# State-space decay exponents: one minimum over four chunks, the column subtracted as the exponential's bias

## The reference, cut to what matters

```python
a_cs = jnp.cumsum((dt * a)...)                   # running sum of the log decay
seg = a_cs[..., :, None] - a_cs[..., None, :]
decay = jnp.exp(jnp.where(causal, seg, -jnp.inf))
cb = jnp.einsum('bclgn,bcsgn->bcgls', cm, bm)
y_diag = jnp.einsum('bcgls,bcgjls,bcsgjp->bclgjp', cb, decay, xdt)
```

## Time and profile before

| | |
|---|---|
| median of 3 runs | 1905.43 us (1902.82 to 1907.98) |
| profiled execution, its own time | 1910.72 us |
| its span, first to last instruction | 1909.1 us |
| PE busy | 1687.8 us, 88% of the span |
| DVE busy | 728.6 us, 38% |
| ACT busy | 374.4 us, 20% |
| POOL busy | 278.9 us, 15% |
| mean granted TensorE clock | 0.951 |

### The profile page before, as it was taken

How to read it: one execution, slowest core, us unless ns; L and a number is a source line. 1 busy time by engine, 2 the same in 40 slices (tenths; PEclk the granted TensorE clock), 3 DMA queues, 4 the chain that set the end, 5 groups by cost and what they waited for, 6 DMA issues and landing times.

```text
span 1909.1 us, 22819 instructions
## 1 busy us (share of the span) xinstructions
PE 1687.8 (88%) x8856; PEld 900.1 (47%) x8857; DVE 728.6 (38%) x1292; ACT 374.4 (20%) x722; POOL 278.9 (15%) x300
## 2 busy tenths in 40 slices
PE   3989799899889889999999999999999867999893
PEld 0554455355355344544454555444656343555441
DVE  1144743754564464620014776214015221222124
ACT  2321232132122122000012333410010121111112
POOL 0003411430530341000000000000000012222122
PEclk9999899999899989999999999999989878999997
DMA  9621101021011116622111001213331645997994
GB/s 314 247 76 44 45 22 45 1 67 44 1 45 45 44 45 220 220 88 89 45 44 44 30 14 45 89 44 104 143 122 45 263 177 205 394 347 291 394 378 152
DMA packets 109537, 242.00 MB, mean 127 GB/s; under 512 B 8505, under 2 KB 18238, under 8 KB 109474
## 3 DMA queue, kind: packets, MB, share of 16 engines
q1 hardware_dynamic: 86800, 180.60, 26.3%
q0 software_dynamic: 14128, 48.51, 7.0%
q10 hardware_dynamic: 8546, 12.03, 1.8%
HBM read 219.10 MB, written 22.02 MB: 126 GB/s over the span
## 4 chain that ended last, share of the span: by engine, by line
PE 75%; DVE 12%; ACT 3%; DMA 3%; issue 3%; POOL 2%; ACTq 2%; DVEq 0%; POOLq 0%; PEldq 0%
PE psum L432 15%; PE psum L1036 8%; PE psum L444 7%; PE psum L722 6%; PE psum L609 4%; PE psum L1058 4%; PE psum L436 4%; PE psum L837 3%; PE psum L667 2%; PE psum L635 2%; PE psum L506 2%; PE psum L454 2%; PE psum L871 1%; PE psum L769 1%; DVE arena L1726 1%
## 5 line engine op out<-in xcount | busy, mean ns | idle before, releaser
L432 PE MATMUL psum<-arena 128*128 128x512 f32 x688 | 312.9, 611 | 10.3 <-issue 4.6
L432 PEld LDWEIGHTS psum<-arena 128*128 128x128 f32 x688 | 132.3, 196 | 171.1 <-issue 163.3
L1036 PE MATMUL psum<-arena 128*32 128x256 f32 x2816 | 166.9, 389 | 1.5 <-DVE arena L2080 1.5
L444 PE MATMUL psum<-arena 128*128 128x512 f32 x352 | 155.2, 600 | 0.1
L609 PE MATMUL psum<-arena 128*128 128x512 f32 x256 | 131.7, 645 | 1.2 <-ACT arena L1230 1.2
L1036 PEld LDWEIGHTS psum<-arena 128*32 128x32 f32 x2816 | 92.2, 111 | 61.2 <-issue 8.5
L722 PE MATMUL psum<-arena 128*128 128x512 f32 x256 | 111.5, 593 | 0.0
L444 PEld LDWEIGHTS psum<-arena 128*128 128x128 f32 x352 | 67.3, 193 | 82.3 <-issue 82.2
L2156 POOL TENSOR_TENSOR arena<-arena 128x512 f32<-128x512 f32 x40 | 49.5, 1248 | 356.5 <-ACT arena L1285 305.6
L2192 POOL TENSOR_TENSOR arena<-arena 128x512 f32<-128x512 f32 x64 | 82.7, 1296 | 101.7 <-ACT arena L1325 101.7
L1682 DVE SCALAR_TENSOR_TENSOR arena<-arena 128x772 f32<-128x772 f32 (+1 forms) x96 | 93.9, 978 | 3.4
(11 more groups left out here) (350 smaller groups left out, 2124.7 us busy)
## 6 DMA issues: line engine op xcount, KB each, us to landing
arena<-exp_w_d SPq DMA_DIRECT2D x48, 2048.0 KB, 17.7
arena<-w_in_d SPq DMA_DIRECT2D x22, 2048.0 KB, 7.9
arena<-ada_w_d POOLq DMA_DIRECT2D x8, 2048.0 KB, 9.1
slots<-arena POOLq DMA_DIRECT2D x1, 9216.0 KB, 27.2
arena<-ada_w_d SPq DMA_DIRECT2D x4, 2048.0 KB, 23.2
arena<-ssd_proj_d SPq DMA_DIRECT2D x4, 2048.0 KB, 9.5
slots<-arena POOLq DMA_DIRECT2D x92, 64.0 KB, 5.0
arena<-slots POOLq DMA_DIRECT2D x22, 256.0 KB, 6.1
```

The costliest lines, as they stand in the source:

```text
L432: ins = mmul(ps[:, 0:T], slot[:, k, m * P:(m + 1) * P], src[:, k, C:NT], start=(k == 0), stop=(k == KD - 1))
L444: ins = mmul(ps[:, 0:n], src[:, k, t * P:(t + 1) * P], slot[:, k, 0:n], start=(k == 0), stop=(k == KD - 1))
L1036: ins = mmul(psU[q * R:(q + 1) * R, 0:2 * HF], XT[:, k % 2, k // 2, :], w13[p][:, :, k, q * HF:(q + 1) * HF], start=(k == 0), stop=(k == K ...
```

## The change

DVE makes a negated copy of `acs` once, in `tmpd[0]` (`nacs`). For each head, DVE's four instructions become one, which takes the minimum of the row and the column, with the column broadcast along each chunk. The exponential adds the negated column as its bias: min(r, a) - a is min(r - a, 0). A bias is one number for each partition, and the four chunks have different ones, so ACT's one exponential of 512 columns becomes four of 128.

```diff
--- before.py
+++ after.py
@@ -154,6 +154,7 @@
         tmpd = [alloc(TT, 2 * SH) for _ in range(2)]
+        nacs = tmpd[0]
@@ -1322,7 +1323,10 @@
                         act.wait_ge(*is_free(("R", g, d, h)))
-                        run(mm[n % NM], mm[n % NM], ACT.Exp).then_inc(S_("decay_ready"), 1)
+                        at = d * SH + g * HPG + h
+                        for c in range(TL):
+                            ins = run(mm[n % NM][:, c, :], mm[n % NM][:, c, :], ACT.Exp, bias=nacs[:, TC + c, at:at + 1])
+                        ins.then_inc(S_("decay_ready"), 1)
@@ -1641,6 +1645,7 @@
             dve.wait_ge(*is_free(("acs",)))
+            step(v.tensor_scalar(nacs, acs, -1.0, None, ALU.mult))
             v.tensor_tensor(wend, tmpd[1], acs, ALU.subtract).then_inc(S_("acs_out"), 1)
@@ -1740,10 +1745,8 @@
-                    for c in range(TL):
-                        ins = v.tensor_scalar(mm[n % NM][:, c, :], bank(key)[:, c * P:(c + 1) * P],
-                                              acs[:, TC + c, at:at + 1], 0.0, ALU.subtract, ALU.min)
-                    ins.then_inc(is_free(key)[0], 1)
+                    v.tensor_tensor(mm[n % NM], bank(key)[:, :].rearrange("p (c l) -> p c l", c=TL),
+                                    acs[:, TC:TT, at:at + 1].to_broadcast([P, TL, P]), ALU.min).then_inc(is_free(key)[0], 1)
```

## The result

| | before | after |
|---|---|---|
| median of 5 runs | 1906.97 us (1902.82 to 1911.38) | 1921.55 us (1918.13 to 1923.15) |
| profiled execution, its own time | 1910.72 us | 1918.13 us |
| its span | 1909.1 us | 1916.5 us |
| DVE busy | 728.6 us | 691.6 us |
| ACT busy | 374.4 us | 414.2 us |

The changed kernel is slower: ratio 1.0066, with a 95% interval from 1.0048 to 1.0084. Two later sets of runs of the same kernel gave 1.0053 [1.0041, 1.0066] and 1.0062 [1.0038, 1.0087]. The forecast was 1907.0, in a range up to 1913. With the 1.6 us that it gave the change, some 9 to 13 us of the 10.9 to 14.6 measured are left that it had not put there.

What follows compares the result with a forecast made beforehand. PE was taken to bound the kernel, feeling the change only at 16 places where it waits. Four groups at +0.30 give +1.2 us, the negated copy +0.4: +1.6 on 1905.43, so 1907.0, range 1901 to 1913.

Steps and rivals of the forecast that it cites:

- The exponentials: ACT, each head: four exponentials of 128 columns take x = 1.29 us against 0.63, 0.66 more.
- that rival: ACT: the four exponentials don't overlap, x = 1.64, sum +7.2 us, 1912.6; chance 0.07.
- Place 1: First head of direction 0: ACT's table load hides the faster minimum, so PE waits 0.66 us more.
- Place 2: Middle of direction 0: the order at the ports turns round, PE's own loop keeps a head at 5.17 us; 0.
- the rival of the relief in the loop: DVE gives 0.44 us back in five heads of each group, 8.8 in all: 1898; chance 0.04.
- Place 3: Last head of direction 0: L1719 no longer stalled, 1.02 us less, chain 0.22 more: -0.80.
- Places 4 and 5: First and last head of direction 1: the longer chain is in the open, +0.22 us each.
- The negated copy: DVE, once, ahead of the split whose end PE waits for: +0.4 us in the open.
- each head's 0.22 reaches PE: Direction 0's middle loops are not closed by PE, 64 x 0.22 = 14 us: 1919.5; chance 0.03.
- the clock goes slower: In two or three groups a 1.2 GHz stretch is added outside cover, 1.8 to 2.7 us each: 1913; chance 0.06.
- the prediction's last sign of being wrong: Profile after: the prediction is wrong if the clock's stretches move.
- The clock goes faster: Moved waits leave the clock high after direction 0's first product, 10.8 us come back: 1896; chance 0.07.

Runs made afterwards that it cites:

- min_alone: Kernel before with DVE's one minimum, but one exponential of 512 columns without bias, so the column is not subtracted: 1898.22 us, 0.9940.
- after_twice_d1: Changed kernel, PE doing the product of the last head but one in direction 1 twice: 1921.93 us, 1.0074 against the kernel before.
- after_pause: Changed kernel, one part of the z projection moved from behind M(6) to behind M(0) in direction 0: 1922.95 us, 1.0055 against the kernel before.
- before_twice_d0: Kernel before, PE doing the product of the last head but one in direction 0 twice: 1912.12 us, 1.0017.
- before_late_first: Kernel before, one unused exponential of 512 columns added on ACT ahead of the first head of direction 0: 1912.66 us, 1.0015.
- before_z_three: Kernel before, three z projection parts ahead of direction 0's first product, none between its last two: 1900.93 us, 0.9962.
- after_z_three: Changed kernel, three z projection parts ahead of direction 0's first product, none between its last two: 1899.76 us, 0.9963 against the kernel before.
- z_three: Order of PE's work with three z projection parts ahead of direction 0's first product, in either kernel: 1900.93 us before the change, 1899.76 after.

## Why the prediction was wrong

Taken by its own steps:

- **DVE's minimum**, 0.69: right (690 ns), and it is not stalled beside POOL.
- **The exponentials**, x = 1.29 from 390 ns and 0.30 apart: 390 ns and 1.28. The overlap between neighbours in place is there; that rival is out. The Trainium skill ("ScalarE: Activation LUTs", What ACT_TABLE_LOAD costs) would give 387 ns and 1.27, and the trace agrees.
- **Place 1**, first head of direction 0, +0.66: from the row to M(0) the four groups took 16.96 and take 19.49, +0.63 a group.
- **Place 2**, the middle, 0: the order of the ports turned as described. The step from one L636 to the next is 5.09 (219.07 to 224.16), not 5.17, so PE's own loop was not quite what closed it; a moved step was one of the prediction's signs of being wrong. `min_alone` shows more of that: M(1) to M(6) lost 1.1 us a group, half of the 2.2 that the rival of the relief in the loop, at 0.04, had given. With the longer exponentials on top, the changed kernel gives none of it back at the end: M(1) to M(6) is 0.51 longer, as the product of the head before the last comes later.
- **Place 3**, last head of direction 0, -0.80: M(6) to M(7) is 1.46 shorter and M(1) to M(6) 0.51 longer, -0.95 together.
- **Places 4 and 5**, +0.22 each: +0.21 for the first; for the last +0.14 in the chain ahead of M(6) and 0.05 in M(6) to M(7), 0.2 together.
- **The negated copy**, +0.4: PE's wait ahead of the scan stage went from 4.3 to 4.7. In the view of waits of the changed kernel (name, count, the longest):

```profile
PE psum L559 <- DVE arena L1660: 4.7, 1, 4.7
```

The sum of these was +1.6; they measured +0.8 to +0.9. Had the time been made of them alone, it would have come out at 1908. So the rival "each head's 0.22 reaches PE" is out as well, though its 1919.5 lies near what was measured: it wanted 3.5 us of waits a group, and there are 0.1.

**The step that failed** is the rival "the clock goes slower", at 0.06 and with 1913 as its time, and behind it the sum of the forecast, which has no term for the clock: it puts at nothing, without a reason, that the stretches at 1.2 GHz could move. They did, by about 10 us of the 11, and the prediction's last sign of being wrong was just that. The rival's mechanism was put right, "if in two or three groups such a stretch is added outside cover": that is what happened, in three groups at the end of direction 1, and in M(0) to M(1) as well. But it was counted at 1.8 to 2.7 for each of two or three, and the open terms came to about 10 us in all. I had looked for such stretches behind the first product only the earlier trace rows. The one at the start of direction 1, which cost nothing, I had not looked for; so I could not ask what happens if it moves.

The Trainium skill ("TensorE: Matmul & The Clock Gate", HAM oscillation) describes a matmul loop in which TensorE waits for a DMA in each round, starts the next round at the lower clock, and pays for it every time. The trace agrees in that the clock falls in every group of both kernels; here TensorE waits for other engines, 0.3 to 1.7 us at a time in rows 8 to 10, and the change moved such waits.

"The clock goes faster" had more chance (0.07) than its opposite, though the prediction said itself that nothing in the change speaks for it, as the wait ahead of the first product gets longer. That spoke for the slower case, and should have moved the chances.

**What is shown, and what isn't.** Shown: the waits sum to less than a microsecond; about 10 us come from stretches at 1.2 GHz, with the same matmuls; three executions of the changed kernel have those of the first groups at the same products, and two of the kernel before have three hidden ones each, which the changed kernel lacks; the cost is gone when PE's waits are filled with its own work. Not shown: which wait decides. `after_twice_d1` and `after_pause` each spoke against one candidate, `before_twice_d0` (1.0017, just clear of no change) and `before_late_first` (1.0015, not clear of it) each changed one wait alone, were about 4 us longer by their medians, and in each another part of the after picture appeared. That the two together make the ten is a guess; it was not tried.

The best versions are `before_z_three` and `after_z_three`, 0.9962 and 0.9963. They differ from the kernels as given by three parts of the z projection (six matmul records a group) put ahead of a wait. The change in question adds nothing to them.

## What to carry to other kernels

Where PE sets the end and still has short waits, a change elsewhere has two prices: the waits, which a timeline gives to a tenth of a microsecond, and where the stretches at 1.2 GHz then fall, which here was ten times as much. So list these stretches with what stands behind each, and if some of them are hidden, give the case that they move a real chance and its full price. And try first what makes both small: work of PE's own ahead of its waits, which was worth 7 us before and some 20 after the change (`z_three`), against at most 10 for the shorter minimum.

## What the runs showed of the hardware

- DVE and POOL exclude each other in both directions. With two operands in SBUF on each side, the one that starts second pays: DVE 1.71 instead of 0.69, or POOL 1.71 instead of 1.27. A difference of 0.1 us in their starts decides which.
- A minimum of 512 columns of PSUM with an SBUF operand broadcast along them takes 690 ns, no more than L1716, which has such an operand too.
- Equal programs repeat their waits ahead of a product (to 0.03 us) and, in these profiles, some of the places of their stretches at 1.2 GHz: in group 0, 6.83 us at the last product of direction 1 in three executions of the changed kernel, 3.41 us at the start of direction 1 in two of the kernel before. Other stretches moved (M(0) to M(1) 25.00 and 19.88 us), and two executions of `after_z_three` differ by 15 us.
